# Pitch of the split weight tiles and of the operand tiles in SBUF, with eight instead of six split slots in the MLP

## The reference

```python
h = rmsnorm(x, g_mix)
proj = h @ w_in                                   # pool | q | k | v, 512 columns each
x = x + concat(pool_mix, moba_attention) @ w_out
x = x + cross_attend(rmsnorm(x, g_cross), mk, mv, w_cq, w_co)   # mk, mv = rmsnorm(mem) @ w_ck, w_cv
hm = rmsnorm(x, g_mlp)
x = x + jnp.square(jax.nn.relu(hm @ w_up)) @ w_down             # D 1024, D_FF 4096
y = rmsnorm(x, g_final)
```

## Time and profile before

| | |
|---|---|
| median of 3 runs | 419.39 us (417.31 to 420.57) |
| profiled execution, its own time | 416.81 us |
| its span in the profile | 414.8 us |
| TensorE matmul busy | 408.8 us (99%) |
| VectorE busy | 253.3 us (61%) |
| ScalarE busy | 226.7 us (55%) |
| granted TensorE clock | 1.0 (2.4 GHz) |

### The profile page before, as it was taken

How to read it: one execution, slowest core, us unless ns; L and a number is a source line. 1 busy time by engine, 2 the same in 40 slices (tenths; PEclk the granted TensorE clock), 3 DMA queues, 4 the chain that set the end, 5 groups by cost and what they waited for, 6 DMA issues and landing times.

```text
span 414.8 us, 8425 instructions
## 1 busy us (share of the span) xinstructions
PE 408.8 (99%) x3372; PEld 383.7 (93%) x3372; DVE 253.3 (61%) x400; ACT 226.7 (55%) x392; POOL 30.4 (7%) x41
## 2 busy tenths in 40 slices
PE   9999999999999999999999999999999999999995
PEld 9999989986879998958899999999999999999995
DVE  5899989666255795543259777766767534454302
ACT  5876958725464574424267666666565443453313
POOL 1003026000000120000022000000000000010010
PEclk9999999999999999999999999999999999999999
DMA  8999958974988966999527536555456555545002
GB/s 284 388 386 364 285 208 253 342 266 168 393 312 315 378 233 235 366 342 344 217 103 253 205 136 195 199 188 171 182 202 204 195 179 186 187 161 184 2 2 104
DMA packets 37257, 96.60 MB, mean 233 GB/s; under 512 B 4186, under 2 KB 13274, under 8 KB 37082
## 3 DMA queue, kind: packets, MB, share of 16 engines
q1 hardware_dynamic: 35106, 92.24, 63.5%
q10 hardware_dynamic: 2112, 3.82, 2.6%
HBM read 91.73 MB, written 4.54 MB: 232 GB/s over the span
## 4 chain that ended last, share of the span: by engine, by line
PE 91%; DMA 3%; DVE 2%; SPq 1%; issue 1%; ACT 0%; DVEq 0%
PE psum L1104 75%; PE psum L826 5%; PE psum L1046 2%; DMA raw<-in_w_in 2%; PE psum L954 2%; PE psum L941 2%; DMA pages<-in_page_table 1%; PE psum L838 1%; PE psum L878 1%; SPq L772 1%; PE psum L887 1%; PE psum L925 1%; PE psum L947 0%; DVE rstd L1586 0%; SPq L767 0%
## 5 line engine op out<-in xcount | busy, mean ns | idle before, releaser
L1392 DVE TENSOR_TENSOR w_lo<-raw,w_hi 128x1024 fp32r<-128x1024 f32 x67 | 82.4, 1239 | 60.6 <-ACT w_hi L1124 60.4
L1124 ACT ACTIVATE w_hi<-raw 128x1024 fp32r<-128x1024 f32 (+1 forms) x73 | 73.9, 1020 | 58.4 <-PE psum L1104 44.8
L1104 PE MATMUL psum<-mix_hi,w_hi 128*128 128x264 f32 (+1 forms) x288 | 82.4, 286 | 0.0
L1104 PE MATMUL psum<-mix_hi,w_lo 128*128 128x264 f32 (+1 forms) x288 | 81.1, 282 | 0.0
L1104 PE MATMUL psum<-mix_lo,w_hi 128*128 128x264 f32 (+1 forms) x288 | 81.1, 282 | 0.0
L1104 PE MATMUL psum<-act_hi,w_hi 128*128 128x264 f32 x232 | 66.4, 286 | 0.3 <-DVE w_lo L1392 0.3
L1104 PE MATMUL psum<-act_lo,w_hi 128*128 128x264 f32 x232 | 65.6, 283 | 0.0
L1104 PE MATMUL psum<-act_hi,w_lo 128*128 128x264 f32 x232 | 65.3, 281 | 0.0
L1104 PEld LDWEIGHTS psum<-mix_hi,w_hi 128*128 128x128 f32 x288 | 54.0, 188 | 0.9 <-issue 0.8
L1104 PEld LDWEIGHTS psum<-mix_lo,w_hi 128*128 128x128 f32 x288 | 54.1, 188 | 0.1
L1104 PEld LDWEIGHTS psum<-mix_hi,w_lo 128*128 128x128 f32 x288 | 54.0, 188 | 0.0
(11 more groups left out here) (208 smaller groups left out, 814.8 us busy)
## 6 DMA issues: line engine op xcount, KB each, us to landing
raw<-in_w_down SPq DMA_DIRECT2D x20, 512.0 KB, 3.4
raw<-in_w_up SPq DMA_DIRECT2D x18, 512.0 KB, 3.9
raw_more<-in_w_up SPq DMA_DIRECT2D x14, 512.0 KB, 3.8
stage<-in_mem_v SPq DMA_DIRECT2D x12, 512.0 KB, 6.3
raw_more<-in_w_down SPq DMA_DIRECT2D x12, 512.0 KB, 4.3
stage<-in_cache_v SPq DMA_DIRECT2D x16, 256.0 KB, 6.6
keysT<-in_cache_k SPq DMA_DIRECT2D x16, 256.0 KB, 4.9
keysT<-in_mem_k SPq DMA_DIRECT2D x8, 512.0 KB, 6.4
```

Source lines behind the costliest of these rows:

```text
L1104: mm = pe.matmul(out, a, b, start=first and m == 0, stop=end_ and m == 2)
L1124: return nc.scalar.activation(out, in_, ACT.Copy, scale=scale)
L1392: V.tensor_tensor(lo_of(c), raw_of(c), hi_of(c).bitcast(F32), ALU.subtract).then_inc(w_lo_ready, 1)
```

## The change

A row tile of split weights gets a pitch of 520 columns (2080 bytes) instead of 512 (2048). An operand row tile goes back from 320 columns (1280 bytes) to 264 (1056). Both pitches are 32 modulo 256. With the room that the operand tiles give back, the MLP has four more split slots instead of two. The empty tensor `beside_operands` shrinks from 1664 to 768 columns. The starts become: `w_hi` 13,440, `w_lo` 30,080, `mix_hi` 46,944, `mix_lo` 55,392, `act_hi` 87,136, `act_lo` 95,584, `w_hi_more` 112,256, `w_lo_more` 128,896, `hid_hi` 145,760, `hid_lo` 179,552.

```diff
-PITCH = 320
-SPLIT, MORE_SPLIT = 4, 2
+SPLIT, MORE_SPLIT = 4, 4
+SHIFT = 8
...
-        w_hi = sb("w_hi", [P, SPLIT, CK, CN], F32R)
-        w_lo = sb("w_lo", [P, SPLIT, CK, CN], F32R)
+        def weights(name, slots):
+
+            return sb(name, [P, slots * CK, CN + SHIFT], F32R)[:, :, 0:CN].rearrange("p (s k) n -> p s k n", k=CK)
+
+        w_hi = weights("w_hi", SPLIT)
+        w_lo = weights("w_lo", SPLIT)
         sb("before_mix", [P, 56])
-        mix_hi = sb("mix_hi", [P, KT, PITCH], F32R)[:, :, 0:T]
-        mix_lo = sb("mix_lo", [P, KT, PITCH], F32R)[:, :, 0:T]
+        mix_hi = sb("mix_hi", [P, KT, T], F32R)
+        mix_lo = sb("mix_lo", [P, KT, T], F32R)
...
-        act_hi = sb("act_hi", [P, KT, PITCH], F32R, early)[:, :, 0:T]
-        act_lo = sb("act_lo", [P, KT, PITCH], F32R, early)[:, :, 0:T]
+        act_hi = sb("act_hi", [P, KT, T], F32R, early)
+        act_lo = sb("act_lo", [P, KT, T], F32R, early)
...
-        sb("beside_operands", [P, 1664])
+        sb("beside_operands", [P, 768])
...
-        w_hi_more = sb("w_hi_more", [P, MORE_SPLIT, CK, CN], F32R)
-        w_lo_more = sb("w_lo_more", [P, MORE_SPLIT, CK, CN], F32R)
+        w_hi_more = weights("w_hi_more", MORE_SPLIT)
+        w_lo_more = weights("w_lo_more", MORE_SPLIT)
         sb("before_hid", [P, 56])
-        hid_hi = sb("hid_hi", [P, FT, PITCH], F32R)[:, :, 0:T]
-        hid_lo = sb("hid_lo", [P, FT, PITCH], F32R)[:, :, 0:T]
+        hid_hi = sb("hid_hi", [P, FT, T], F32R)
+        hid_lo = sb("hid_lo", [P, FT, T], F32R)
```

## The result

The changed kernel takes 419.06 us, the median of 14 runs (418.07 to 420.39), against 417.75 us for the kernel before (14 runs, 417.26 to 420.57). The ratio is 1.003, with a 95% interval of 1.0017 to 1.0043: 1.3 us slower, less than 1% but clear of the noise.

What follows compares the result with a forecast made beforehand. It took TensorE's own matmul pace to bound the kernel. Slots 0, neighbours +1.2, writes 0 and take-out 0 gave 418.0 us against 416.81 profiled, or 420.6 us on the 419.39 median; range 415.0 to 427.0 us.

Steps and rivals of the forecast that it cites:

- The bound: TensorE at its own pace in the whole MLP: 1392 matmuls in 167.04 us, 0.1200 us each, without waits.
- The slots at 0: Eight split slots in the MLP remove no wait, since TensorE never waits for a split there: 0 us.
- The own weights keep 224: Each streamed row tile and its matmul's own weights stay 224 apart modulo 256, in all pairs of tensors.
- The next weights, +1.2 us: Neighbouring float32r matmuls: 555 pairs at 192 cost 0.0015 us each, 341 at 0 cost 0.001 each.
- At difference 224 and at 32 alike: Every float32r stream runs some 8% under the rate taken from plain matmuls, w_cv at 32 like 264 columns at 224.
- Wider writes at 0: Splits writing 2 x 512 elements at a distance cost nothing more, as the count is the same; at worst 0.3 us.
- The take-out of chunk 55: Chunk 61's extra split delays the take-out by 1.7 us, but TensorE does not wait: 0 us.
- The number: Whole kernel: 418.0 us on the profiled execution, 420.6 us on the median of the runs shown.
- the rival of the slower pace: Next weights' difference matters much: 425.6 us at half price, 431.8 at the highest rows; chance 0.18.
- The faster pace: Float32r matmuls at changed pairs gain up to 0.009 us each, at most down to 411.3 us; chance 0.12.
- late take-out: Chunk 61's load lands late and TensorE stands 2.3 us before chunk 58: 423.2 us; chance 0.06.
- the deeper buffer: More split slots help after all, through MLP waits the chain does not show; 0 us, no chance of its own given.

Runs made afterwards that it cites:

- slots_only: The kernel before with its pitches of 2048 and 1280 bytes, but seven split slots in the MLP instead of six: 417.57 us, 0.9995 times the kernel before.
- layout_only: The changed kernel's layout with all eight split slots, but splits placed and held back as with six: 418.74 us, 1.002 times the kernel before.
- all_shifted_32: The kernel before with 32 empty bytes ahead of the weight tiles, every difference still 224: 417.83 us in one execution.
- diff_192_0_128: The kernel before with other empty columns: difference 192 for mix, 0 for act, 128 for hid; 417.14 us in one execution, beside 417.37 for the kernel before.
- mix_192: The kernel before with difference 192 for the mix tiles and 224 for act and hid, by empty columns alone: 417.45 us, 0.9986 times the kernel before.
- diff_0_128_64: The kernel before with other empty columns: difference 0 for mix, 128 for act, 64 for hid; 420.36 us in one execution, beside 417.37 for the kernel before.

## Why the prediction was right or wrong

**The bound.** Right. TensorE sets its own pace in the MLP, and the whole loss is a change of that pace. The stretch is inside the 167 to 169 us that I gave for it.

**The slots at 0.** Right, shown by slots_only (0.9995) and from the other side by layout_only, which keeps the pace of 167.93 us without the earlier splits.

**The own weights keep 224.** Right as arithmetic, and worth keeping: the operand pitch alone made the stretch 169.80 us.

**The next weights, +1.2 us.** This is the step whose mechanism failed. The sum was near by luck: its prices came from single rows that are rounded to 0.01 us, for other kinds of weights. I priced each pair at 192 with 0.0015 us and each at 0 with 0.001 us, as if these differences were dearer in themselves. Held constant in the MLP, both run at 0.1200 us. In the changed kernel the matmuls of such pairs are followed after 119.6 ns, sooner than the 120.0 of before; it is those behind a change that are late: by the starts, 121.0 to 121.3 ns on average for the matmuls with passes one and two. I had said that a cost would show behind the third and sixth matmul. It shows behind the first, second, fourth and fifth. (These are means over both row tiles. In the kernel before, the distances alternate between 118 and 122 ns; each pass has both, and so a mean of 120.0.) The term measured 2496 x 0.00063 = 1.6 us in pace, and 1.3 us in the medians. The single rows of 0.13 and 0.14 us that I took for the upper ends are no price of a difference: with the same addresses, the matmul at 52.73 us of slots_only is followed after 0.122 us where the one at 52.81 was after 0.130, and in all_shifted_32, with the same differences, the one at 149.09 after 0.120 where the one at 148.94 was after 0.136. What made them is open.

**"At difference 224 and at 32 alike."** This reading led me to think that differences hardly matter. It compared a stream of 264 columns with one of 512. The right comparison is the same matmul at other differences: w_cv took 233.1 ns at 32, and 229.3 at 64 (diff_192_0_128); w_up 120.0 at 224 and 126.7 at 96. The rule of the Trainium skill that I weighed ("SBUF — State Buffer", section "Who interferes with whom": two independent read ports, neither slows the other) would make this term 0. These runs do not agree with that: with nothing changed but empty columns, the difference between the two operands moved the pace by up to 5.6% (0.1267 against 0.1200 us). Whether it is the two ports that hinder each other, no run shows.

**Wider writes at 0.** Right: 1.22 us a split on VectorE in the row above, 1.06 on ScalarE.

**The take-out of chunk 55.** Right in its outcome, TensorE does not wait; the delay was 1.1 us where I had worked out 1.7, and the slack left for chunk 58 was 229.86 - 228.51 = 1.4 us instead of 0.7.

**The number.** Here the step that failed is the base: I put the sum on the median of the three runs shown, 419.39 us, and forecast 420.6, though the profiled execution at 416.81 us gave 418.0 for the same sum. The kernel before has 417.75 us over 14 runs, so that base was 1.6 us high, more than the whole effect. The step from one kernel to the other was forecast at +1.2 us and measured at +1.3; the absolute number is 1.5 us too high for the base alone. And since the expected step was under a third of the 1% bound, "within 1%" held, but it says little: the change is a real loss of 0.3%, which 14 runs of each kernel tell from none.

**The rivals.** Of the rival of the slower pace the place is right, the pairs with other next weights, and the price far off: 1.6 us of pace where it had 6.2, and 12.4 at the highest. The faster pace did not come on 264 columns. There was no late take-out, and the deeper buffer does not help.

## What to carry to other kernels

When a stream of matmuls has no waits, divide a long stretch of the chain by its count: a pace off by half a percent shows there at once, where the means per instruction (282 or 283 ns before, 284 after) leave it open whether the starts moved. If the layout of SBUF is free to choose, and the operands are float32r on 264 columns as here, hold the difference between the streamed operand and the weights constant, modulo 256, for the matmul's own weights and for the next ones alike, and try a few values with empty columns. Pitches that are multiples of 256 bytes do this; a scheme that shifts both sides together keeps only the own pair, and then a loop with fewer changes of the row tile gets most of it back.

## What the runs showed of the hardware

The pace of float32r matmuls is not set by their columns alone. On 264 columns the runs show 120.0, 120.9, 121.4, 121.7, 122.2, 123.3 and 126.7 ns from start to start, each held over many matmuls. On 256 columns w_ck sat at 113.3 or at 117.8 ns per matmul, chunk by chunk, in one and the same run with the difference 192 throughout (mix_192). The distances between single starts, in whole ns, repeat a pattern of their own: 118 and 122 in turn at 224, a steady 120 at 192, 0 and 128, and 126, 124, 116, 120, 121 over and over where 0 ran at 121.4.

The same difference can have two paces. In diff_192_0_128 the act tiles at difference 0 ran at 120.0 ns through the eight chunks of w_out, and at some 121.3 in most of w_in and w_co; the mix tiles at 0 in diff_0_128_64 ran at 121.4 in w_cq and the first chunks of w_up and at 120.0 in the rest of w_up. There the pace held until other matmuls, those at L860, came between. That looks like two streams, the operand's and the next weights', which lock to each other, and which a change of their difference throws out of step; the runs show the paces and the loss at a change, but no run shows the mechanism, and it stays open. Of the eight differences tried, 224 alone was at 120.0 ns in every stretch of 264 columns.
